# Channel LayerNorm statistics as one row on 128 partitions in a two-layer conv and pool trunk

## The reference

```
u_b = b_v * sigmoid(b_g)
u_b = causal_depthwise_conv(u_b, conv_b_w, conv_b_b)      # 31 taps, 512 channels
u_b = silu(layer_norm(u_b, ln_b_g, ln_b_b))               # LayerNorm over the 512 channels
y_b = u_b * silu(b_z)
...
y   = concatenate([y_a, y_b, y_c])                        # 1536
out = layer_norm(ALPHA * x + y @ w_out, ln_g, ln_b)       # over 1024
```

## Time and profile before

| | |
|---|---|
| median of 3 runs | 790.82 us (790.62 to 790.99) |
| the profiled execution | 790.98 us, of which span of the slowest core 789.4 us |
| spans of the eight cores | 787.3 to 789.4 us |
| mean granted clock of the cores | 0.993 to 0.996 |
| PE busy | 767.9 us (97%) |
| DVE busy | 484.1 us (61%) |
| ACT busy | 380.0 us (48%) |
| GpSimd busy | 306.6 us (39%) |
| DMA | 108.59 MB |

### The profile page before, as it was taken

The page is one execution under the profiler, slowest core; times in us unless marked ns, Lnnn a source line. Parts: engine busy times, 40 slices in busy tenths (PEclk is TensorE's granted clock), DMA queues, the critical chain, the costliest instruction groups (busy, mean ns, idle before and its releaser), DMA issues.

```text
span 789.4 us, 16350 instructions; the slowest of 8 cores (787.3 to 789.4 us)
## 1 busy us (share of the span) xinstructions
PE 767.9 (97%) x5215; PEld 408.5 (52%) x5269; DVE 484.1 (61%) x769; ACT 380.0 (48%) x631; POOL 306.6 (39%) x379
## 2 busy tenths in 40 slices
PE   8899999999999999999999999999999999999994
PEld 7556666654444444445555566666444444444441
DVE  1322268986656577455655657975665654887467
ACT  1222367555545584354454478546433447635421
POOL 4121148864011146346111016945501113783393
PEclk9999999999999999999999999999999999999998
DMA  8877889987987864654797895994646677342022
GB/s 123 162 152 144 177 136 167 149 129 176 212 209 188 186 138 62 94 70 82 129 213 179 180 216 103 154 174 72 133 112 178 159 194 187 54 67 28 1 99 115
DMA packets 77060, 108.59 MB, mean 138 GB/s; under 512 B 24496, under 2 KB 46000, under 8 KB 76464
## 3 DMA queue, kind: packets, MB, share of 16 engines
q0 software_dynamic: 28944, 61.22, 46.5%
q1 hardware_dynamic: 48032, 46.31, 22.2%
HBM read 116.78 MB, written 16.78 MB: 169 GB/s over the span
## 4 chain that ended last, share of the span: by engine, by line
PE 92%; issue 3%; DMA 2%; DVE 2%; POOL 0%; ACT 0%; DVEq 0%; ACTq 0%; POOLq 0%
PE ps L556 60%; PE ps L1135 20%; PE ps L709 8%; DMA xT<-xint 2%; PE ps L753 1%; PE ps L739 1%; PE ps L948 1%; DVE mem L591 1%; DVE xT L591 1%; DVE mem L928 0%; DVE mem L586 0%; PE ps L537 0%; ACT mem L582 0%; POOL wrg L497 0%; PE ps L1058 0%
## 5 line engine op out<-in xcount | busy, mean ns | idle before, releaser
L556 PE MATMUL ps<-xT,wrg 128*128 128x512 bf16 (+7 forms) x2790 | 515.4, 339 | 3.7 <-issue 1.4
L556 PEld LDWEIGHTS ps<-xT,wrg 128*128 128x128 bf16 x2816 | 272.1, 98 | 229.7 <-issue 13.7
L582 ACT ACTIVATE mem<-ps 128x512 f32<-128x512 f32 (+12 forms) x284 | 131.3, 484 | 181.1 <-PE ps L556 140.4
L586 POOL TENSOR_TENSOR yb<-mem 128x512 bf16<-128x512 f32 (+3 forms) x120 | 129.0, 1081 | 130.4 <-ACT mem L582 57.8
L1135 PE MATMUL ps<-wo,yb 128*128 128x512 bf16 x743 | 174.7, 379 | 1.1
L497 POOL DMA_DIRECT2D wrg<-w_in_r x144 | 80.4, 561 | 204.0 <-PE ps L556 131.2
L582 ACT ACT_TABLE_LOAD x72 | 92.4, 1283 | 62.8 <-DVE mv L1173 46.5
L1135 PEld LDWEIGHTS ps<-wo,yb 128*128 128x128 bf16 x768 | 75.0, 98 | 86.3 <-issue 0.7
L582 ACT ACTIVATE mem<-mem,par 128x384 f32<-128x384 f32 (+3 forms) x80 | 57.4, 727 | 70.1 <-DVE mem L586 62.2
L591 DVE SCALAR_TENSOR_TENSOR Rb<-Rb,ps 128x512 f32<-128x512 f32 (+1 forms) x59 | 40.2, 681 | 73.2 <-PE ps L1135 72.3
L591 DVE SCALAR_TENSOR_TENSOR mem<-mem,par 128x384 f32<-128x384 f32 (+3 forms) x80 | 66.0, 826 | 14.5 <-ACT mem L582 10.1
(11 more groups left out here) (70 smaller groups left out, 383.4 us busy)
## 6 DMA issues: line engine op xcount, KB each, us to landing
wrg<-w_in_r POOLq DMA_DIRECT2D x144, 256.0 KB, 5.5
mem<-mem SPq DMA_DIRECT2D x64, 135.0 KB, 3.2
Rb<-xin SPq DMA_DIRECT2D x16, 512.0 KB, 5.1
x1s<-Rb POOLq DMA_DIRECT2D x16, 512.0 KB, 4.5
Rb<-x1s SPq DMA_DIRECT2D x13, 512.0 KB, 5.0
mem<-mem SPq DMA_DIRECT2D x64, 103.0 KB, 4.9
wo<-w_out_r POOLq DMA_DIRECT2D x24, 256.0 KB, 9.0
out<-Rb POOLq DMA_DIRECT2D x8, 512.0 KB, 3.3
```

Of the source, the lines that this page charges most:

```text
L556: o = P.add("pe", lambda e, kk=kk: e.matmul(bk.ap[:, 0:N], lhsT=wrg_t[:, s, kk, :], rhs=xT(kk, tok0, N), start=(kk == 0), stop=(kk == 7)), ...
L582: return P.add("act", lambda e: e.activation(out=out, in_=in_, func=func, **kw), reads=reads, writes=writes, cost=cost).fin
L586: return P.add(eng, lambda e: e.tensor_tensor(out=out, in0=in0, in1=in1, op=op), reads=reads, writes=writes, cost=0.15 + n * (0.0022 if en ...
```

## The change

`lnb` gets another way to mean and reciprocal root; the rest is costs.

- The four squares are all taken before the sums. PE makes eight matmuls of 32 output columns (L746): the plain sum in column strip 0 (partitions 0 to 31 of one bank) and the sum of squares in strip 1 (partitions 32 to 63), alternating. One PSUM bank instead of two.
- ACT copies the 64 partitions, scaled by 1/512, into `m`. Two DMAs on SP (L774) take partition 0 and partition 32, one row of N values each, and lay it on N/k partitions with k (2 to 4) values each, in the new tile `tiny`.
- DVE squares the mean and subtracts, ACT takes the root, DVE the reciprocal, on k values per partition.
- Two DMAs (L789) write mean and reciprocal root as rows to the new DRAM tensor `lnrows`, and two more (L795) read each row back into all 128 partitions of `m` and `rs`.
- The planner's costs: an activation with a bias is dearer by 0.08 us, or 0.16 with a scale too; `copy` 0.4 us instead of 0.25; a memset 0.25 instead of 0.1; the gate and two A operations dearer per element (`more`); 0.1 us at either end of a conv group.

The diff, cut to its core:

```diff
-            yield from square(0)
-            f = yield from square(1)
+            for g in range(4):
+                f = yield from square(g)
             yield f + 1.5
-            yield lambda: spare(2)
             Ps = yield from new_bank()
-            Pq = yield from new_bank()
...
+            def sums(g):
+                for i, x in enumerate((cbs[g], sqb[g])):
+                    o = P.add("pe", lambda e, i=i, x=x: e.matmul(
+                        Ps.ap[32 * i:32 * i + 32, 0:N], lhsT=ones_t[:, 32 * i:32 * i + 32], rhs=x.ap, start=(g == 0), stop=(g == 3),
+                        tile_position=(0, 32 * i)), reads=[R_ones] + x.res, writes=Ps.res if (g, i) in ((0, 0), (3, 1)) else [],
+                        cost=mmc(N) / 2 + 0.015 + (0.1 if (g, i) in ((0, 0), (3, 1)) else 0.0))
...
-            act(rs.ap, Ps.ap[:, 0:N], AF.Square, Ps.res, rs.res, scale=1.0 / 512, psum=True)
-            f = stt(rs.ap, Pq.ap[:, 0:N], 1.0 / 512, rs.ap, ALU.mult, ALU.subtract, Pq.res + rs.res, rs.res, psum=True)
-            f = act(rs.ap, rs.ap, AF.Sqrt, rs.res + [R_eps], rs.res, bias=eps_t[:, 0:1])
-            f = P.add("dve", lambda e: e.reciprocal(out=rs.ap, in_=rs.ap), reads=rs.res, writes=rs.res, cost=0.1 + 0.0064 * N).fin
-            t0 = f - 1.0
+            f = act(m.ap[0:64], Ps.ap[0:64, 0:N], AF.Copy, Ps.res, m.res, scale=1.0 / 512, psum=True)
+            for i in range(2):
+                row = m.ap[32 * i:32 * i + 1, 0:N]
+                row = bass.AP(row.tensor, row.offset, [row.ap[0], [k, r], [1, k]])
+                o = P.add("sp", lambda e, i=i, row=row: e.dma_start(out=ty[:, i], in_=row), reads=m.res, writes=[Ry[i]], dma=True,
+                          cost=0.6, land=0.3)
+            yield o.fin + 1.0
+            small(lambda e: e.tensor_tensor(out=ty[:, 2], in0=ty[:, 0], in1=ty[:, 0], op=ALU.mult), Ry[:1], Ry[1:])
+            f = small(lambda e: e.tensor_tensor(out=ty[:, 1], in0=ty[:, 1], in1=ty[:, 2], op=ALU.subtract), Ry[1:], Ry[1:])
+            f = act(ty[:, 2], ty[:, 1], AF.Sqrt, Ry[1:] + [R_eps], Ry[1:], bias=eps_t[0:r, 0:1])
+            f = small(lambda e: e.reciprocal(out=ty[:, 1], in_=ty[:, 2]), Ry[1:], Ry[1:])
+            for i in range(2):
+                row = ln_d[il, i, 0:N].rearrange("(p c) -> p c", c=k)
+                o = P.add("sp", lambda e, i=i, row=row: e.dma_start(out=row, in_=ty[:, i]), ... cost=0.6, land=0.3)
+            yield o.fin + 1.0
+            for i, x in enumerate((m, rs)):
+                row = bass.AP(row.tensor, row.offset, [[0, 128], [1, N]])
+                o = P.add("sp", lambda e, x=x, row=row: e.dma_start(out=x.ap, in_=row), ... cost=0.6, land=1.0)
+            f = o.fin + 2.0
+            t0 = f
...
+            if bias is not None and n > 1:
+                cost += 0.08 + (0.08 if scale is not None else 0.0)
```

More of the change, by code:

```diff
@@ L371, in build_nc @@
         st_t = sb("stt", [128, 2, 2, 6], F32)
+        ty_t = sb("tiny", [128, 4, 3, 4], F32)
         mv_t = sb("mv", [128, 2, 4], F32)
@@ L393, in build_nc @@
         R_ini = mk("ini", 2)
+        R_ty, R_lm, R_ln = [mk("ty%d_" % i, 2) for i in range(4)], mk("lm", 4), mk("ln", 4)
         R_x1 = mk("x1_", NBLK * 8)
@@ L734, in square @@
             def square(g):
-                sqb[g] = yield from take(Z_SQ + 1024 * rot("sq", 2), BF16, N)
+                sqb[g] = yield from take((Z_SQ, Z_SQ + 1024, Z_X + 2048, Z_X + 3072)[g], BF16, N)
                 return act(sqb[g].ap, cbs[g].ap, AF.Square, cbs[g].res, sqb[g].res)
-            def sqmm(g):
-                o = P.add("pe", lambda e: e.matmul(Pq.ap[:, 0:N], lhsT=ones_t[:], rhs=sqb[g].ap, start=(g == 0), stop=(g == 3)),
-                          reads=[R_ones] + sqb[g].res, writes=Pq.res if g in (0, 3) else [], cost=mmc(N))
+            def sums(g):
[4 more added lines that the diff above has]
+                        cost=mmc(N) / 2 + 0.015 + (0.1 if (g, i) in ((0, 0), (3, 1)) else 0.0))
                 sqb[g].free()
@@ L755, in lnb @@
[L755 to L765 removed]
+                f = sums(g)
             lnb_busy[0] = False
             yield f
[L768 removed]
@@ L772, in lnb @@
             yield f
-            f = P.add("dve", lambda e: e.reciprocal(out=rs.ap, in_=rs.ap), reads=rs.res, writes=rs.res, cost=0.1 + 0.0064 * N).fin
+            f = small(lambda e: e.reciprocal(out=ty[:, 1], in_=ty[:, 2]), Ry[1:], Ry[1:])
+            yield f + 0.3
+            for i in range(2):
+                row = ln_d[il, i, 0:N].rearrange("(p c) -> p c", c=k)
+                o = P.add("sp", lambda e, i=i, row=row: e.dma_start(out=row, in_=ty[:, i]), reads=[Ry[i]], writes=[R_ln[il]] if i else [R_lm[il]],
+                          dma=True, cost=0.6, land=0.3)
@@ L774, in lnb @@
+            yield o.fin + 1.0
+            for i, x in enumerate((m, rs)):
+                row = ln_d[il, i, 0:N]
+                row = bass.AP(row.tensor, row.offset, [[0, 128], [1, N]])
+                o = P.add("sp", lambda e, x=x, row=row: e.dma_start(out=x.ap, in_=row), reads=[R_lm[il], R_ln[il]][i:i + 1], writes=x.res,
+                          dma=True, cost=0.6, land=1.0)
+            ln_free.append(il)
+            f = o.fin + 2.0
             left = [4]
-            t0 = f - 1.0
+            t0 = f
```

43 lines of the change are left out of this document (21 added, 22 removed).

## The result

The changed kernel took 833.23 us in the median (831.32 to 835.78, 4 runs), the kernel before 790.74 us beside it. The ratio is 1.0536, 95% interval [1.0508, 1.0564]. The forecast was 786.1 us with a range to 790.6. The profiled execution of after spans 830.5 us on its slowest core, 41.1 us more than the 789.4 before; the eight cores lie between 823.9 and 830.5, so nothing is due to one core.

The account below looks back on a forecast made before the run. PE's instruction stream was taken to bound the kernel (busy 97% of 789.4 us). Span 789.4 - 5.7 (sums) + 1.0 (waits) = 784.7 us, plus 1.6 less 0.2 gives 786.1 us; range 784.2 to 790.6.

Parts of the forecast that it names:

- Spread traffic: 20 DMAs reading rows back to 128 partitions, 4.2 MB on 108.6 MB: weight loads delayed a little, cost 0.
- They have the 27 us of slack just named: Weight loads: nine slots, some 35 us of PE ahead of 7.5 us landings, so small delays cost 0.
- PE's waits, 1.0 us (0 to 7): PE waiting behind DVE, GpSimd and SP queues held by late hops, taken as 6 us each in block one, 4 later.
- B: Rival: in the first block, hops of 7 to 8 us hold DVE and PSUM banks; 3 to 5 us, 789 us; chance 0.21.
- C: Rival: late hops block queues in every block, slower than before; +9 us, 794 us; chance 0.11.
- Sums side by side: LayerNorm sums on PE, strips paired: 6.98 us saved, 1.27 us for added strip changes, net 5.7 us less.
- D: Rival: the two strips of the sums run one after the other; 792.1 us plus waits; chance 0.04.
- E: Rival: paired strips overlap only partly, 2.2 us on top of the forecast, 788.3 us; chance 0.06.
- all of it is on the path: The net 5.7 us taken from PE by pairing the sums shortens the kernel in full.
- Refitted estimates: Planner's dearer costs shift operations by a place or two everywhere: 0, with -1 to +2 us in the range.
- DVE -33 us and ACT -11 us: Reciprocals, subtractions, a Square and full-tile Sqrt leave DVE and ACT; worth 0 on PE, only cover for what is added.
- Tail 10.6 us, head unchanged: Head to 36 us and last eleven projection groups keep their order, so early waits and the 10.6 us tail stay.

Follow-up runs that it names:

- no_hop_small: Changed kernel, same order, no compute engine waiting for the 60 added DMAs, each cut to 2 to 4 numbers of one partition; 794.52 us, ratio 1.0028.
- no_hop_wait: Changed kernel, same order and all 60 added DMAs at full size, but compute engines read constants and wait for none of them; 824.99 us, ratio 1.0409.
- whole_rows: Changed kernel, values right, without pieces: variance, root and reciprocal along the row on 32 partitions, each row stored as one piece and spread; 801.29 us, ratio 1.0121.
- rows_whole: Changed kernel, no engine waiting for the chain, first DMAs tiny, a constant row stored as one piece, spreads reading `lnrows`; 797.47 us, ratio 1.0065.
- spread_one: Changed kernel, no engine waiting for the chain, first two hops tiny, 128 partitions reading one row of an input; 794.46 us, ratio 1.0028.
- spread_own: Changed kernel, no engine waiting for the chain, first two hops tiny, each partition reading its own row of an input; 794.40 us, ratio 1.0025.
- hop2_pieces: Changed kernel, no engine waiting for the chain, first hop tiny, DRAM store in 96 or 128 pieces, spreads reading an input; 819.97 us, ratio 1.0353.
- strips_only: Kernel before with its sums in column strips of one PSUM bank and all four squares first, without the added DMAs; 797.1 us, ratio 1.006.
- hybrid: Units 0 and 3 compute LayerNorm as the kernel before, units 1 and 2 without pieces, refitted estimates kept; 789.71 us against 792.34, ratio 0.9973.

## Why the prediction was wrong, step by step

In shares of the kernel before, the loss of 5.4% is made of: order and pairing 0.3% (no_hop_small), traffic 3.8% (no_hop_wait less that), waits for the chain 1.3% (after less no_hop_wait). In us: 2, 30 and 10. The shares hold for this order of taking away; waits without the traffic are likely to be shorter (whole_rows, with its chain, is 0.6% above rows_whole, where nothing waits). The forecast had -5.7, 0 and 1.0 for them.

- *Spread traffic, "0"*: the step that failed, and 30 us of the 47 between forecast and result. It counted bytes, 4.2 MB on 108.6, and for the spread that is right (spread_one, spread_own). It left out hops one and two, since 1 to 2 KB are no bytes to speak of, and gave no reason why their traffic should be free. 40 DMAs of that size, 20 of which write 96 or 128 pieces side by side into DRAM, cost 21 us, and reading the row buffer behind them 9 more.
- *"They have the 27 us of slack just named"*: the slack of the weight slots was eaten: without any wait for the chain, PE waited 13.9 us for weights (no_hop_wait). `wo` and x go through the same queue. A load of 1024 KB of x takes 16.2 us in place of 11.1 (25.1 in hop2_pieces), a load of `wo` 17.6 in place of 9.0, and the weights stand in that queue.
- *PE's waits, 1.0 us (0 to 7)*: some 10 us by subtraction. Mechanism and place were right (DVE held at 140 to 165 us, PE L559 behind it, as B and C name it), the hops were mis-sized: I took 6 and 4 us from transfers of 18 to 103 KB, and the store of 1.5 KB took 11.2.
- *Clock*: no term. The sum assumed that a wait costs its own length. Six waits of 2.1 to 6.6 us had stretches at the lower granted clock in or behind them, some 13 us of PE's time.
- *Sums side by side, -5.7 us*: the price was right (0.98 us a group), rivals D and E fell. The estimate for a pair that the prediction worked out from the Trainium skill ("TensorE: Matmul & The Clock Gate", in its section on why this matters for kernels: 2.38 times for three column tiles) was 0.27 us; measured are 0.216. Less the 12.9 us of the lower clock, PE's busy time is 762.8 us, 5.1 below before, so the work did leave. That "all of it is on the path" was wrong: strips_only is 4.7 us slower than before, no_hop_small 2.2. A gain came only where the new order was kept out of units 0 and 3 (hybrid).
- *Refitted estimates, 0*: right (0.9989).
- *DVE -33 us and ACT -11 us, worth 0*: the worth was right; whole_rows puts that work back and is faster. The sizes were not: with the forecast's 6 us for the small operations DVE should have lost 27 us, and its busy time fell by 8.3 (484.1 to 475.8), ACT's by 7.4. The small operations took some 7 us, and others grew longer: the gate multiplication over 512 columns from 1.01 to 1.33 us in the mean. So there was less cover than the prediction counted on.
- *Tail 10.6 us, head unchanged*: right. PE's last group ends at 820.0 us, 10.5 us before the end.
- *Rival C, 0.11*: the sign was its own, "slower", and so was the blocking of queues in more than unit 0, but its mechanism (late hops alone) was priced at 794 us. Traffic that slows other loads was in no rival.

What stays open: what the DMA engines or the memory do with neighbouring small writes, and whether it takes all eight cores writing at once; how far apart pieces must lie; why hop two alone costs more than both hops; and by what steps the new order of the sums makes mixer C late in unit 0, which was placed but not taken apart; why DVE's gate multiplications grew longer.

## What to carry to other kernels

Price a DMA by what it writes, not only by its bytes: a row stored to DRAM from many partitions in pieces of 8 to 16 bytes that touch one another held up other transfers, most of all where the engines were full, while the same bytes in one piece, or the same pieces 512 bytes apart, were nearly free. Where DMA engines are 90% busy, ask of an added transfer whose landing it delays, and look for a share that rises while the GB/s fall. And moving work off an engine that had slack gained nothing; here the reciprocals were cheaper left alone.

## What the runs showed of the hardware

- 20 writes of 1 to 2 KB in pieces of 8 to 16 bytes side by side in DRAM cost 26 us on an 8-core kernel of 792 us with 20 reads of 128 to 256 KB beside them, and 2 us when the pieces began 512 bytes apart. From SBUF to SBUF pieces of that size cost 3 us at most.
- 128 partitions that read one row of DRAM cost no more than 128 that read their own (1.0028 against 1.0025).
- Two column strips of 32 at 512 columns run at the pace of one full matmul, as four do: 0.98 us from first start to next start for eight matmuls in two strips and for 16 in four (strips_only), 0.12 us of it for leaving the strips.
- The granted clock fell to its lower level (0.50) in or behind six waits of 2.1 to 6.6 us in the middle of a dense stream, and not behind three others of 2.0 to 2.5 us; that cost some 13 us, beside 33 us of waits.
